# The merged attention rows turned by VectorE squares and regrouped through device memory, in place of TensorE transposes

## The reference, cut to what matters

```
merged = sigmoid(ga) * (ya @ w_oa) + sigmoid(gb) * (yb @ w_ob)     # [256, 2048]
x = x + g1 * (merged @ w_out)
h2 = rms_norm(x, norm2_w) * (1 + sc2) + sh2
ff = (silu(h2 @ w_ffn_gate) * (h2 @ w_ffn_up)) @ w_ffn_down
x = x + g2 * ff
```

## Time and profile before

| | us |
|---|---|
| median of 3 runs | 2201.3 (2200.71 to 2202.82) |
| profiled execution, its own time | 2199.33 |
| span of that execution in the trace | 2197.6 |
| PE busy in the span | 2176.8 |

### The profile page before, as it was taken

The page is one execution under the profiler, slowest core; times in us unless marked ns, Lnnn a source line. Parts: engine busy times, 40 slices in busy tenths (PEclk is TensorE's granted clock), DMA queues, the critical chain, the costliest instruction groups (busy, mean ns, idle before and its releaser), DMA issues.

```text
span 2197.6 us, 32142 instructions
## 1 busy us (share of the span) xinstructions
PE 2176.8 (99%) x10822; PEld 1840.4 (84%) x10822; DVE 1508.1 (69%) x2039; ACT 1015.4 (46%) x1246; POOL 297.0 (14%) x554
## 2 busy tenths in 40 slices
PE   9999999999999999999999999999999999999998
PEld 7898888988877887898888888888888888888886
DVE  5766668877777877597786768776666666554544
ACT  5445545454444446444555544454444444443433
POOL 2101110113220010701110211111112111000000
PEclk9999999999999999999999999999999999999999
DMA  8867577778986584968766886767878887775563
GB/s 292 246 194 239 173 259 249 193 231 291 308 295 182 165 304 142 251 217 264 225 187 192 285 278 237 237 222 237 267 256 277 266 262 240 224 231 182 189 200 137
DMA packets 204124, 512.25 MB, mean 233 GB/s; under 512 B 32696, under 2 KB 59992, under 8 KB 203744
## 3 DMA queue, kind: packets, MB, share of 16 engines
q1 hardware_dynamic: 166256, 394.10, 56.1%
q0 software_dynamic: 37456, 115.95, 16.6%
q10 hardware_dynamic: 288, 0.52, 0.1%
HBM read 502.61 MB, written 7.91 MB: 232 GB/s over the span
## 4 chain that ended last, share of the span: by engine, by line
PE 87%; DMA 5%; DVE 4%; ACT 2%; issue 2%; POOLq 0%; SPq 0%; DVEq 0%; ACTq 0%; POOL 0%
PE ps L2300 72%; PE ps L2344 9%; DMA ada_raw<-in_w_ada_dram 3%; DMA raw<-in_ml_w_in_dram 2%; DVE lo L1269 1%; DVE acc_s L1281 1%; PE ps L2397 1%; PE ps L2768 1%; PE ps L2757 1%; ACT hi L713 1%; PE ps L2658 0%; DVE acc_g L1281 0%; PE ps L2492 0%; PE ps L2493 0%; DVE conv_tmp L1751 0%
## 5 line engine op out<-in xcount | busy, mean ns | idle before, releaser
L1269 DVE TENSOR_TENSOR lo<-raw,hi 128x1024 fp32r<-128x1024 f32 x731 | 890.2, 1223 | 580.0 <-ACT hi L713 577.6
L713 ACT CAST hi<-raw 128x1024 fp32r<-128x1024 f32 x731 | 765.4, 1051 | 1010.2 <-PE ps L2300 765.0
L2300 PE MATMUL ps<-hi,XH 128*128 128x512 f32 x1944 | 607.9, 393 | 4.3 <-DVE lo L1269 2.1
L2300 PE MATMUL ps<-lo,XH 128*128 128x512 f32 x1944 | 601.9, 389 | 0.0
L2300 PE MATMUL ps<-hi,XL 128*128 128x512 f32 x1944 | 601.5, 389 | 0.0
L2300 PEld LDWEIGHTS ps<-hi,XL 128*128 128x128 f32 x1944 | 364.9, 188 | 76.6
L2300 PEld LDWEIGHTS ps<-lo,XH 128*128 128x128 f32 x1944 | 364.9, 188 | 76.5
L2300 PEld LDWEIGHTS ps<-hi,XH 128*128 128x128 f32 x1944 | 361.4, 188 | 80.4 <-issue 3.9
L607 POOL DMA_DIRECT2D ada_raw<-in_w_ada_dram x320 | 172.3, 539 | 1184.9 <-DVE acc_s L1281 893.5
L1281 DVE SCALAR_TENSOR_TENSOR acc_s<-ada_raw,c_act,acc_s 128x512 f32<-128x512 f32 x256 | 191.0, 746 | 24.6 <-DMA ada_raw<-in_w_ada_dram 23.5
L2344 PE MATMUL ps<-XH,hi 128*128 (+1 forms) x504 | 142.9, 284 | 0.0
(11 more groups left out here) (387 smaller groups left out, 1891.6 us busy)
## 6 DMA issues: line engine op xcount, KB each, us to landing
ada_raw<-in_w_ada_dram POOLq DMA_DIRECT2D x384, 256.0 KB, 4.6
raw<-in_w_in_dram SPq DMA_DIRECT2D x136, 512.0 KB, 4.5
raw<-in_ml_w_in_dram SPq DMA_DIRECT2D x128, 512.0 KB, 4.7
raw<-in_w_gate_dram SPq DMA_DIRECT2D x176, 256.0 KB, 3.0
raw<-in_w_up_dram SPq DMA_DIRECT2D x176, 256.0 KB, 3.5
raw<-in_w_down_dram SPq DMA_DIRECT2D x88, 512.0 KB, 3.8
raw<-in_mla_w_in_dram SPq DMA_DIRECT2D x47, 512.0 KB, 4.8
raw<-in_mla_w_out_dram SPq DMA_DIRECT2D x32, 512.0 KB, 4.6
```

The lines of the kernel that those rows point to most:

```text
L713: nc.scalar.copy(hi[:, j, :], raw[:, j, :]).then_inc(hi_ready, 1)
L1269: nc.vector.tensor_tensor(lo[:, j, :], raw[:, j, :], hi[:, j, :].bitcast(F32), ALU.subtract) \
L2300: ins = mm(ps[:, o:o + HALF], x, w[:, b % RING, c0:c0 + HALF], start=first, stop=(k == n_rows - 1 and x is xl), skip_group_check=True)
```

## The change

The diff, cut to its core. `mTa` and `mTb` leave `TURN_PLAN`; `merged` is turned in three parts, `m0` (columns 0 to 1023), `m1a` and `m1b` (512 columns each). The 48 sums from `oa0` to `wo1` are dealt 7, 8, 5, 2, 13, 13 in place of 6, 6, 6, 6, 12, 12.

```diff
-    "ga0@0:act ga1@0:act gb0@0:act gb1:act oa0:dve ob0:dve oa1:dve ob1:dve mTa:split4 wo0:dve mTb:split4 wo1@0:dve "
+    "ga0@0:act ga1@0:act gb0@0:act gb1:act oa0:dve ob0:dve oa1:dve ob1:dve wo0:dve wo1@0:dve "
...
-              "qa": 8, ..., "oa0": 6, "ob0": 6, "oa1": 6, "ob1": 6, "wo0": 12, "wo1": 12}
+              "qa": 8, ..., "oa0": 7, "ob0": 8, "oa1": 5, "ob1": 2, "wo0": 13, "wo1": 13}
...
+        MERGED = {"m0": (0, 8), "m1a": (8, 4), "m1b": (12, 4)}
...   POOL
+            def regroup(name, dst, src, scratch):
+                n = src.shape[1] // 4
+                pool.wait_ge(*squares_of(name))
+                if REGROUPED.index(name):
+                    pool.wait_ge(rows_moved, 80 * REGROUPED.index(name))
+                pool.dma_start(scratch, src).then_inc(rows_moved, 16)
+                pool.wait_ge(rows_moved, 80 * REGROUPED.index(name) + 16)
+                for c in range(4):
+                    part = scratch.rearrange("(a i) n -> i a n", a=4)[:, :, c * n:(c + 1) * n]
+                    pool.dma_start(dst[32 * c:32 * c + 32, :].rearrange("p (a n) -> p a n", a=4), part) \
+                        .then_inc(rows_moved, 16)
...
-            ada_units(12, 20)
-            pool.wait_ge(*complete("mTa"))
+            ada_units(12, 17)
+            for name in MERGED:
+                if name != "m1b":
+                    ada_to(ADA_FIRST["ob1" if name == "m0" else "wo0"] + RING)
+                regroup(name, merged_part(merged_regrouped, name), merged_part(merged_turned, name),
+                        merged_part((merged_rows[0], merged_rows[1]), name))
+            ada_to(16 * 20)
             init_acc(acc_g[:, :], 5 * D, D, 24)
...   ACT
+            def merged_hi(name):
+                act.wait_ge(*rows_of(name))
+                if name == "m1a":
+                    act.wait_ge(ev("m_split"), 1)
+                nc.scalar.copy(operand_part_of(XH, name), quarters(merged_part(merged_regrouped, name)))...
+            merged_hi("m0")
+            first4(B_WO)
+            rest_blocks(B_WO, 4, 8)
+            merged_hi("m1a")
+            rest_blocks(B_WO, 8, 10)
+            merged_hi("m1b")
+            rest_blocks(B_WO, 10, 16)
...   DVE
+            def turn_squares(dst, src, f):
+                n = f * TOK * 32
+                for c in range(4):
+                    ins = nc.vector.transpose(
+                        dst[:, c * n:(c + 1) * n].rearrange("p (f t e) -> p f t e", f=f, t=TOK),
+                        src.rearrange("p t (f c e) -> p c f t e", c=4, e=32)[:, c])
+                ins.then_inc(ev("squares_turned"), 1)
...   in the loop over oa0, ob0, oa1, ob1; n == 2 is oa1
+                if n == 2:
+                    dve.wait_ge(ev("merged"), 2)
+                    turn_merged("m0")
                 if n < 3:
                     rest(n0, 8, ("ob0", "oa1", "ob1")[n])
+                if n == 2:
+                    split_merged("m0", 1)
+            merge_columns("ob1", 1, (ev("ob1_first"), 1))
+            dve.wait_ge(ev("merged"), 4)
+            turn_merged("m1a")
+            lo_block(B_WO + 3, 3)
+            turn_merged("m1b")
+            rest_blocks(B_WO, 4, 8, 16, "wo0")
+            split_merged("m1a", 2)
...
-            rest_blocks(B_WO, 8, 16, 16, "wo0")
+            rest_blocks(B_WO, 8, 10, 16, "wo0")
+            split_merged("m1b", 3)
+            rest_blocks(B_WO, 10, 16, 16, "wo0")
...   PE
-            transposes("mTa", operand_tiles(merged[0], 0))
-            token_major("wo0", B_WO, 16, XH, XL, m_tiles, blocks=(0, 5), first_free=(ev("ob1_first"), 1))
-            transposes("mTb", operand_tiles(merged[1], 0))
-            token_major("wo0", B_WO, 16, XH, XL, m_tiles, blocks=(5, 16))
+            token_major("wo0", B_WO, 16, XH, XL, lambda k: (ev("m_split"), max(k // 4, 1)),
+                        first_free=(ev("ob1_first"), 1))
             token_major("wo1", B_WO + 16, 16, XH, XL, half_done=True)
```

More of the change, by code:

```diff
@@ L40 @@
 FFN_PASSES = D_FF // HALF
+REGROUPED = ("m0", "m1a", "m1b",) + tuple(f"ffn{_p}" for _p in range(FFN_PASSES))
 PACK = {}
@@ L123 @@
 BANKS_BEFORE = {_name: 4 * _n for _n, _name in enumerate(
-    ("cT", "x1Ta", "x1Tb", "yTa", "yTb", "hTa", "hTb", "mTa", "mTb", "h2Ta", "h2Tb"))}
+    ("cT", "x1Ta", "x1Tb", "yTa", "yTb", "hTa", "hTb", "h2Ta", "h2Tb"))}
 TURN_COUNT = {}
@@ L132 @@
               "mo_1": 20, "mz0": 6, "mz1": 6, "lo0": 8, "lo1": 10,
-              "qa": 8, "kb": 12, "vb": 16, "ga0": 12, "ga1": 12, "gb0": 12, "gb1": 16, "oa0": 6, "ob0": 6, "oa1": 6,
-              "ob1": 6, "wo0": 12, "wo1": 12}
+              "qa": 8, "kb": 12, "vb": 16, "ga0": 12, "ga1": 12, "gb0": 12, "gb1": 16, "oa0": 7, "ob0": 8, "oa1": 5,
+              "ob1": 2, "wo0": 13, "wo1": 13}
 for _p in range(1, 9):
@@ L240, in two_block_kernel, with merged_part, operand_part_of @@
         merged = sig_a
+        merged_turned = (at("merged_turned0", 72, [P, 2 * COLS]), at("merged_turned1", 144, [P, 2 * COLS]))
+        merged_regrouped = (at("merged_regrouped0", 56, [P, 2 * COLS]), at("merged_regrouped1", 128, [P, 2 * COLS]))
+        merged_rows = nc.dram_tensor("merged_rows", [2, P, 2 * COLS], F32, kind="Internal").ap()
+        MERGED = {"m0": (0, 8), "m1a": (8, 4), "m1b": (12, 4)}
+        def merged_part(ms, name):
+            k, n = MERGED[name]
+            return ms[k // 8][:, k % 8 * SEQ:(k % 8 + n) * SEQ]
+        def operand_part_of(m, name):
+            k, n = MERGED[name]
+            return by_quarter(m, k // n, n)
         FH = at("FH", 112, [P, KF, SEQ], F32R)
@@ L361, in two_block_kernel, with squares_of, rows_of @@
         THREES = ("mo1", "down1")
+        def squares_of(name):
+            return ev("squares_turned"), REGROUPED.index(name) + 1
+        def rows_of(name):
+            return rows_moved, 80 * (REGROUPED.index(name) + 1)
         def half_of(name):
@@ L617, in ada_units, with ada_to @@
                         four(u, g, True)
+                ada_sent[0] = 16 * u1
+            ada_sent = [0]
+            def ada_to(m1):
+                for m in range(ada_sent[0], min(m1, 16 * N_UNITS)):
+                    u, k = divmod(m, KD)
+                    if m >= RING:
+                        pool.wait_ge(ada_used, m - RING + 1)
+                    pool.dma_start(ada_raw[:, m % RING, :], w_ada[0][k * P:(k + 1) * P, u * HALF:(u + 1) * HALF]) \
+                        .then_inc(ada_landed[m % RING], 16)
+                    ada_sent[0] = m + 1
+            def regroup(name, dst, src, scratch):
[9 more added lines that the diff above has]
+                        .then_inc(rows_moved, 16)
             def init_acc(acc, b0, n, zeroed):
@@ L1163, in _ @@
                 rest(B_MERGE + 72 + 8 * n, 8)
[L1164 to L1176, removed]
+            def merged_hi(name):
+                act.wait_ge(*rows_of(name))
+                if name == "m1a":
+                    act.wait_ge(ev("m_split"), 1)
+                nc.scalar.copy(operand_part_of(XH, name), quarters(merged_part(merged_regrouped, name)))                   .then_inc(ev("m_hi"), 1)
+            merged_hi("m0")
[5 more added lines that the diff above has]
+            rest_blocks(B_WO, 10, 16)
             first4(B_WO + 16)
@@ L2208, in ffn_product @@
                 dve.wait_ge(product_done, p + 1)
-                for c in range(4):
-                    src = tmp[:, :].rearrange("p (t f c e) -> p c f t e", t=TOK, c=4, e=32)[:, c]
-                    ins = nc.vector.transpose(squares_turned[:, p, c * SEQ:(c + 1) * SEQ]
-                                              .rearrange("p (f t e) -> p f t e", f=4, t=TOK), src)
-                ins.then_inc(ev("ffn_turned"), 1)
+                turn_squares(squares_turned[:, p, :], t, 4)
             def ffn_lo(p):
```

54 lines of the change are left out of this document (15 added, 39 removed).

## The result

The changed kernel takes 2230.15 us (median; 2225.72 to 2234.26) against 2201.01 of before in the same rounds: a ratio of 1.0139, 95% interval [1.0125, 1.0153]. It is slower, by twice the forecast's 14 us, and above the range. The profiled execution took 2228.87 us, its span is 2227.0, 29.4 above that of before.

What follows compares the result with a forecast made beforehand. PE, busy 99% of the span, was taken to bound the kernel with its own instructions. -3.77 + 5.3 + 5.5 + 6.3 + 2.9 = +16.2 us on the profiled 2199.3 gave 2215.5; range 2206 to 2223 for 8 in 10.

Steps and rivals of the forecast that it cites:

- the three places: PE waits at the start of `wo0`, at block 9 of `wo0` and at the start of `wo1`: 5.3, 5.5 and 6.3 us.
- The transposes: `mTa` with its wait (2.10) and `mTb` (1.67) leave PE: 3.77 us gained, the whole of the possible gain.
- Squares, write: Start of `m0`'s chain: DVE's squares taken as 2.7 us, POOL's 1 MB write until the loads begin as 5.5.
- Loads of `m0`: Four 256 KB loads: last issued 1.66 us after the first, landing taken as 5.5 (3.0 to 7.4); with write, 12.7.
- S: Moment when ACT's cast and DVE's subtraction of `m0` are done, forecast at 1365.8.
- S + 2.4 to PE's start: Start of `wo0`: behind the split DVE does half of `ob1` and block 0's `lo`, 2 x 1.15; PE starts at 1368.2.
- Squares of `m1a` at S + 9.5: DVE after S: both halves of `ob1`, three `lo`, two additions, then `m1a`'s squares (1.43), done at S + 9.5.
- Block 9: In `wo0`, the fifth sum's load queues behind `m1b`'s trip on POOL, delaying the `lo`: PE waits 5.5 us (2.2 to 11).
- The bank: Start of `wo1`: it shares PSUM group 0 with `wo0`, so PE waits 6.3 us for DVE's reading (5.8 to 7).
- The clock: PE's clock falls behind long waits: 1.3 us lost at block 9 and 1.6 at `wo1`, 2.9 together; nothing at `wo0`.
- long trips: Rival: all transfers share the DMA engines with SP's 512 KB blocks and land near 7.4; +23 us, 2222; chance 0.11.
- The rule of the Trainium skill weighed there: DMA time is 2.0 us plus bytes at 436 GB/s; by it `m0`'s trip is 8.7 and `wo0` starts 4 us earlier.

Runs made afterwards that it cites:

- the kernel with whole rows: Against the changed kernel with SP's `wo0` blocks held back until `m0`'s rows landed: `m0`'s four loads fetch 32 whole rows of 8 KB each; 2226.1 us, one execution.
- the first kernel with 7 and 19 sums: Changed kernel with early `m0` squares, other `wo0`/`wo1` groups, `m1` writes back to back, casts behind blocks 9 and 11, 7 and 19 sums for 13 and 13; 2207.3 us.

## Why the prediction was wrong

The direction, the three places and the holders named were right; block 8, where the forecast had no wait, held PE for 1.76. The failed step is the size of the trips: "bounds 3.0 and 7.4, taken 5.5" for the landing of `m0`'s loads, and "a trip of 512 KB is 3.9 + 1.66 + 4.4 = 10.0" for `m1a`. In their place the last of `m0`'s loads landed 11.6 after its issue and the trips took 18.5 and 15.4. With SP's weights held back `m0`'s trip took 12.3, against 12.7 forecast: the weights beside it are the whole of that miss. Against the profiled execution the forecast is 13.4 us low (2228.87 - 2215.5); by steps:

- *The transposes*, -3.77: right; no wait took their place at the seam where rows came in time.
- *Squares, write*: 2.48 (taken 2.7) and 5.25 from write to loads (5.5): right. These 2.48 are also DVE's time for as much as sixteen transposes; the 1.43 that the prediction set against PE's 1.67 is for half as much. No term of the sum used it.
- *Loads of `m0`*: the last was issued at 1355.48 + 1.66 = 1357.14 and landed by 1368.74, 11.6 after it. That is outside the bounds, which came from 128 KB loads that were not beside a burst of weights. The trip is 18.5 in place of 12.7, and S, the end of its split, lies at 1372.96, or 1371.4 without the 1.6 lost ahead: 5.6 late.
- *S + 2.4 to PE's start*: right (1375.33 - 1372.96 = 2.37). *Squares of `m1a` at S + 9.5*: right (1382.4).
- *Block 9*: the price of 5.5 and the measured 6.36 agree only by chance. The chain was due at S + 32.1 and came at S + 37.9: 5.8 late, since `m1a`'s trip took 15.4 in place of 10.0 (2.42 of pause between POOL's first and second load, and 7.5 for the last landing in place of 4.4) and the sum's load 5.0 in place of 4.6. `m1b`'s trip, at 9.7, was as taken. PE came late itself, by the clock at `wo0` and 1.76 at block 8, where the forecast gave `m1a` 2 us to spare; that is why the wait looks small.
- *The bank*: 6.10 of 6.3, right.
- *The clock*: 1.85 and 1.9, 3.75 in place of 2.9: the upper bound of half the wait is not reached, the middle is passed. The 2.55 at `wo0` cost nothing of their own, as forecast: they only shorten the wait at block 9, whose end POOL's chain sets.

5.6 + 5.8 + 0.85 - 0.2 and the 1.6 ahead make 13.65, of 13.4. The rival "long trips" was the near one, and still low, as its landing of 7.4 was. The rule of the Trainium skill weighed there ("DMA: Bandwidth & Descriptors", Anatomy of one DMA) gave an estimate of 2.6 for a load of 256 KB: 5.1 with the weights held back and 9.3 beside them were measured, and the measurements decide. The range failed since both trips erred to the same side, and its bounds had been read where the engines had more room. For `m0` the full DMA engines are shown as the cause. For `m1a` they are argued: they were 0.87 to 0.99 busy from 1388 to 1396, but no run took the traffic beside it away, and 2.42 of its 5.4 too many are the pause; in the kernel with whole rows, where `m1a`'s loads follow one another without it, the trip took 12.6. The warning stood in the earlier trace rows: a share of 0.91 before 4 MB were added.

## What to carry to other kernels

Where PE is at 99%, work taken off it is won only if the way round is hidden: follow the chain from the last producer to the first consumer, and price its transfers in the stretch where they will run, with what SP loads there, not by landings read where the engines have room. Three more places to look at: what stands behind a new wait in an in-order queue of DMA issues (the fifth sum here), the parity of the PSUM groups when an entry leaves the plan, and the clock behind each wait. A regrouping that goes back 32 partitions at a time pays for it in its loads: here 5.1 us each, against 4.0 for as many bytes into 128 partitions.

## What the runs showed of the hardware

- Loads into 32 partitions, with two loads of sums beside them, filled the DMA engines (share 0.97 to 1.03) at 213 to 246 GB/s, with pieces of 2 or of 8 KB; the write of the same bytes from 128 partitions went at 393 (the row of 1350 to 1352 with the weights held back).
- The clock stayed at 1.00 after PE's waits of 1.70 to 2.68 in eight kernels, but fell to 0.50 after one of 2.38 (first PE, then the stretch, of the first kernel with 7 and 19 sums), one of 2.46 and two of 2.02 and 0.82 close together; so how long PE stood in one wait does not by itself decide.

```profile
1392.28 0.70 PE L2394 MATMUL ps<-hi,XH 128*128 128x512 f32 x2 [2.38 <-DVE XL L2200]
```

```profile
1394.00:1396.00 2.00, 2.00 (x6) 1.53 (x5) 1.04 (x1) 1.88 (x2) 0.54 (x1) 0.50 1.02 395
```

- Between POOL's first and second load of `m1a` lies a pause of 2.41 or 2.42 that waits for nothing the profile shows, in all but one of the kernels here whose trips of `m1a` and `m1b` run one behind the other. In that one, with whole rows, the loads follow one another, and the write of `m1b` comes 3.0 after `m1a`'s rows are there (1391.32 to 1394.35; 0.5 in the changed kernel). Its cause stays open.
